# The end of a fused model kernel: two norm weight rows loaded narrow and spread by TensorE, three more weight chunks loaded in halves, a scatter moved between two halves, and a table load moved ahead of a branch

## The reference

```
h = layer_norm(DEEPNORM_ALPHA * h + t, ln_g[i, 0], ln_b[i, 0])
f = moe_ffn(h, ...)        # 32 experts, 4 chosen for each token
h = layer_norm(DEEPNORM_ALPHA * h + f, ln_g[i, 1], ln_b[i, 1])

# one expert, for the rows that chose it:
h = xb @ w_gu[e] + b_gu[e]                      # 1024 -> 2048, gate and up
h_gate, h_up = jnp.split(h, 2, axis=-1)
act = min(h_gate, 7) * sigmoid(1.702 * min(h_gate, 7)) * (clip(h_up, -7, 7) + 1.0)
y = act @ w_down[e] + b_down[e]                 # 1024 -> 1024
```

## Time and profile before

| what | value |
|---|---|
| median of 3 runs | 2072.09 us (2069.9 to 2073.24) |
| span of the profiled execution, first to last instruction | 2072.4 us |
| device time of the profiled execution | not listed apart from its span |
| PE busy | 1989.1 us, 96% of the span |
| DVE, ACT, POOL busy | 43%, 33%, 2% |
| DMA read from HBM | 601.71 MB |

### The profile page before, as it was taken

The page is one execution under the profiler, slowest core; times in us unless marked ns, Lnnn a source line. Parts: engine busy times, 40 slices in busy tenths (PEclk is TensorE's granted clock), DMA queues, the critical chain, the costliest instruction groups (busy, mean ns, idle before and its releaser), DMA issues.

```text
span 2072.4 us, 28104 instructions
## 1 busy us (share of the span) xinstructions
PE 1989.1 (96%) x12146; PEld 1377.3 (66%) x12146; DVE 897.4 (43%) x1078; ACT 688.3 (33%) x949; POOL 39.1 (2%) x30
## 2 busy tenths in 40 slices
PE   8999999999999998999999999999999999999997
PEld 8998768999999886999888544443334333434433
DVE  6766666676666787666644311111111111111102
ACT  5546475545555565444344111110101010101101
POOL 0700000000000000000000000000000000000000
PEclk9999999999999998999999999999999999999999
DMA  9663707556556442555387999999999999999997
GB/s 311 202 218 135 234 1 256 191 184 201 171 189 208 166 159 79 171 199 183 100 294 292 371 427 428 428 428 427 427 428 427 427 428 428 427 428 428 427 428 308
DMA packets 165592, 604.26 MB, mean 292 GB/s; under 512 B 9324, under 2 KB 102464, under 8 KB 140564
## 3 DMA queue, kind: packets, MB, share of 16 engines
q1 hardware_dynamic: 165328, 602.79, 74.9%
q10 hardware_dynamic: 164, 0.04, 0.0%
HBM read 601.71 MB, written 1.09 MB: 291 GB/s over the span
## 4 chain that ended last, share of the span: by engine, by line
PE 69%; DMA 22%; DVE 4%; ACT 3%; issue 1%; SPq 0%; DVEq 0%; ACTq 0%
PE ps L1794 14%; PE ps L1796 14%; PE ps L1795 14%; PE ps L2332 11%; PE ps L2356 6%; DMA sb_raw<-in_moe_w_gate_up 5%; DMA sb_raw<-in_moe_w_down 5%; DMA sb_w_free<-in_moe_w_gate_up 3%; DMA sb_late_raw<-in_moe_w_down 3%; DMA sb_nat_more<-in_moe_w_gate_up 3%; PE ps L2302 2%; DMA sb_w_free<-in_moe_w_down 2%; ACT sb_w_hi L663 1%; DVE sb_w_lo L1084 1%; PE ps L2364 1%; PE ps L2313 1%
## 5 line engine op out<-in xcount | busy, mean ns | idle before, releaser
L1084 DVE TENSOR_TENSOR sb_w_lo<-sb_raw,sb_w_hi 128x2048 fp32r<-128x2048 f32 x175 | 403.0, 2311 | 239.4 <-ACT sb_w_hi L663 238.9
L663 ACT ACTIVATE sb_w_hi<-sb_raw 128x2048 fp32r<-128x2048 f32 x179 | 340.5, 1912 | 168.8 <-PE ps L1796 155.2
L1794 PE MATMUL ps<-sb_xT_hi,sb_w_hi 128*128 128x256 f32 x1344 | 373.3, 278 | 0.0
L1795 PE MATMUL ps<-sb_xT_lo,sb_w_hi 128*128 128x256 f32 x1344 | 372.7, 277 | 0.0
L1796 PE MATMUL ps<-sb_xT_hi,sb_w_lo 128*128 128x256 f32 x1344 | 372.7, 277 | 0.0
L1795 PEld LDWEIGHTS ps<-sb_xT_lo,sb_w_hi 128*128 128x128 f32 x1344 | 253.0, 188 | 1.5
L1794 PEld LDWEIGHTS ps<-sb_xT_hi,sb_w_hi 128*128 128x128 f32 x1344 | 252.3, 188 | 1.7 <-DVE sb_w_lo L1084 0.2
L1796 PEld LDWEIGHTS ps<-sb_xT_hi,sb_w_lo 128*128 128x128 f32 x1344 | 253.1, 188 | 0.0
L1672 DVE COPY sb_h_rows<-ps 128x512 f32<-128x512 f32 x31 | 21.4, 692 | 318.3 <-PE ps L2332 318.3
L1003 ACT ACTIVATE sb_h_rows<-ps 128x512 f32<-128x512 f32 x32 | 19.2, 599 | 420.4 <-PE ps L2332 420.4
L1794 PE MATMUL ps<-sb_w_hi,sb_xT_hi 128*128 128x512 f32 x384 | 153.6, 400 | 0.3 <-DVE sb_xT_lo L1113 0.2
(11 more groups left out here) (314 smaller groups left out, 2541.1 us busy)
## 6 DMA issues: line engine op xcount, KB each, us to landing
sb_raw<-in_moe_w_gate_up SPq DMA_DIRECT2D x49, 2048.0 KB, 34.6
sb_w_free<-in_moe_w_gate_up SPq DMA_DIRECT2D x46, 2048.0 KB, 34.6
sb_raw<-in_moe_w_down SPq DMA_DIRECT2D x23, 2048.0 KB, 34.0
sb_raw<-in_ffn_w_up SPq DMA_DIRECT2D x44, 1024.0 KB, 5.4
sb_raw<-in_ffn_w_down SPq DMA_DIRECT2D x44, 1024.0 KB, 5.1
sb_w_free<-in_moe_w_down SPq DMA_DIRECT2D x22, 2048.0 KB, 33.8
sb_raw<-in_ffn_w_gate SPq DMA_DIRECT2D x43, 1024.0 KB, 5.5
sb_late_raw<-in_moe_w_gate_up SPq DMA_DIRECT2D x17, 2048.0 KB, 32.5
```

Of the source, the lines that this page charges most:

```text
L663: sc.activation(w_hi[:, c % CUT, :], raw[:, c % RAW, :], ACT.Copy).then_inc(hi_made, 1)
L1084: ve.tensor_tensor(w_lo[:, c % CUT, :], raw[:, c % RAW, :], w_hi[:, c % CUT, :].bitcast(F32), ALU.subtract).then_inc(lo_made, 1)
L1794: pe.matmul(o, l_hi, r_hi, start=start, stop=False)
L1795: pe.matmul(o, l_hi, r_lo, start=False, stop=False)
```

## The change

- The two weight rows of the last layer norm are loaded as two DMAs of 4 KB each into partitions 64 and 65 of a tile `narrow_rows`, whose first 32 partitions now hold `down_bias`. They are issued right behind `down_bias`, long before the experts end. The two 512 KB DMAs, and the wait in front of them, go.
- TensorE spreads a row over all partitions by a matmul of K = 2 with a broadcast column of `ident` (`spread_last_rows`): the gain into banks 2 and 3 between chunks t+1 and t+2, the bias into banks 0 and 1 behind the branch. ScalarE copies the spread gain to `xs_even` (128x1024), and the next `turn_picks` waits for that copy. The bias is read from PSUM by VectorE, which waits for it in front of the second pass of the first 128 tokens.
- Chunks t+3, t+4 and t+5 are loaded as two DMAs of 1 MB each, and TensorE waits for the halves apart.
- The scatter of expert 30 moves from behind chunk t+6 to between its halves.
- `warm(ACT.Sqrt)` moves from behind ScalarE's branch to ahead of it.

```diff
 # SP, last_loads
-                for j in range(4):
+                for j in range(3):
                     expert_chunk("gate_up", N_E - 1, j, t + j, laps)
-                for j in range(2):
-                    expert_chunk("down", N_E - 2, j, t + 4 + j, laps)
+                sp.wait_ge(chunk_used, used_no(t + 3, laps) - RING)
+                sp.dma_start(dst[:, 0:1, :], src[:, 0:1, :]).then_inc(last_gate_row, 16)
+                sp.dma_start(dst[:, 1:2, :], src[:, 1:2, :]).then_inc(slot_loaded[(t + 3) % RING], 16)
...
+                sp.dma_start(dst[:, 0:2, :], src[:, 0:2, :]).then_inc(down_rows_0, 16)
+                sp.dma_start(dst[:, 2:4, :], src[:, 2:4, :]).then_inc(slot_loaded[(t + 4) % RING], 16)
...
+                sp.dma_start(dst[:, 0:2, :], src[:, 0:2, :]).then_inc(down_rows_1, 16)
+                sp.dma_start(dst[:, 2:4, :], src[:, 2:4, :]).then_inc(slot_loaded[(t + 5) % RING], 16)
 # SP, behind the router's logits
-            sp.dma_start(down_bias[:], a["moe_b_down_2"][0]).then_inc(down_bias_loaded, 16)
+            sp.dma_start(down_bias, a["moe_b_down_2"][0]).then_inc(down_bias_loaded, 16)
+            sp.dma_start(ln1_rows[0:1, :], a["ln_g_2"][0, 1:2]).then_inc(ln1_loaded, 16)
+            sp.dma_start(ln1_rows[1:2, :], a["ln_b_2"][0, 1:2]).then_inc(ln1_loaded, 16)
 # SP, behind all chunks
-            sp.wait_ge(chunk_used, ROUND_C * more + (MOE_C0 + KEPT_T[1] + 1))
-            sp.dma_start(ln1_gain, rows(a["ln_g_2"][0, 1], D)).then_inc(ln1_loaded, 16)
-            sp.dma_start(ln1_bias, rows(a["ln_b_2"][0, 1], D)).then_inc(ln1_loaded, 16)
 # VectorE, last_layer_norm
+                ln1_bias = ps[:, 0:2, :].rearrange("p a b -> p (a b)")
-                ve.wait_ge(ln1_loaded, 16 * 2)
+                ve.wait_ge(gain_copied, more + 1)
                 ve.scalar_tensor_tensor(out=x[:, 0, :], in0=rows(0), scalar=mean_var[:, 0, 0:1], in1=ln1_gain,
...
+                ve.wait_ge(bias_spread, 1)
                 ve.scalar_tensor_tensor(out=x[:, 0, :], in0=x[:, 0, :], scalar=stat[:, 6:7], in1=ln1_bias,
 # TensorE
+            def spread_last_rows(row, bank):
+
+                one = ident[2 * N_E:2 * N_E + 2, 2 * N_E + row:2 * N_E + row + 1].to_broadcast([2, SLOTS])
+                for h in range(2):
+                    for half in halves:
+                        ins = pe.matmul(ps[half, bank + h, :], one, ln1_rows[:, 512 * h:512 * (h + 1)], start=True, stop=True)
+                return ins
...
             with pe.If(more > 0):
                 with pe.Fori(1, more + 1) as r:
                     another_round(r)
+            spread_last_rows(1, 0).then_inc(bias_spread, 1)
```

More of the change, by code:

```diff
@@ L163, in build @@
         late = ExitStack()
-        down_bias = sb("down_bias", [N_E, D], stack=late)
+        narrow_rows = sb("narrow_rows", [P, D], stack=late)
+        down_bias, ln1_rows = narrow_rows[0:N_E, :], narrow_rows[2 * N_E:2 * N_E + 2, :]
         y_part = ExitStack()
@@ L228, in build @@
         m_sig, m_u, m_u_last = gate_part, up_part, up_last
-        ln1_gain, ln1_bias = kept_more[:, 0, 0:D], kept_more[:, 0, D:2 * D]
+        ln1_gain = xs_even[:].rearrange("p k e s -> p (k e s)")
         halves_of = lambda t: t.rearrange("p (k n) -> p k n", k=2)
@@ L307, in build @@
         out_stored, third_row = sem("out_stored"), sem("third_row")
+        last_gate_row, down_rows_0, down_rows_1 = sem("last_gate_row"), sem("down_rows_0"), sem("down_rows_1")
+        gain_spread, gain_copied, bias_spread = sem("gain_spread"), sem("gain_copied"), sem("bias_spread")
         last_sum, last_mean = sem("last_sum"), sem("last_mean")
@@ L888, in last_layer_norm @@
             def last_layer_norm(more):
-                rows, unread = ps[:, 6:8, :].rearrange("p a b -> p (a b)"), xs_even[:].rearrange("p k e s -> p (k e s)")
+                rows, unread = ps[:, 6:8, :].rearrange("p a b -> p (a b)"), kept_0[:, 0:D]
                 sc.wait_ge(last_scattered, 4 * more + 4)
@@ L1036, in last_two @@
                 turned_picks(e, 0)
+                sc.wait_ge(gain_spread, r + 1)
+                sc.activation(ln1_gain, ps[:, 2:4, :].rearrange("p a b -> p (a b)"), ACT.Copy).then_inc(gain_copied, 1)
                 sc.wait_ge(m_act_made, e + 1)
@@ L1043, in last_two @@
                 turned_picks(e + 1, 1)
+                warm(ACT.Sqrt)
             def last_outputs(r):
@@ L1073, in _ @@
                     another_round(r)
-            warm(ACT.Sqrt)
             last_outputs(more)
@@ L2323, in bias, with gate_up_rows @@
                               bias_parts[:, col + 512 * h:col + 512 * (h + 1)], start=True, stop=False)
-            def gate_up_rows(left, t, j, laps, r):
-                pe.wait_ge(slot_loaded[t % RING], loaded_no(t, laps, r))
+            def gate_up_rows(left, t, j, laps, r, in_halves=False):
+                if in_halves:
+                    pe.wait_ge(last_gate_row, 16 * (r + 1))
+                else:
+                    pe.wait_ge(slot_loaded[t % RING], loaded_no(t, laps, r))
                 for k in range(2):
+                    if in_halves and k == 1:
+                        pe.wait_ge(slot_loaded[t % RING], loaded_no(t, laps, r))
                     for bank in range(2):
@@ L2337, in _, with down_rows @@
             last_own = lambda i: m_u_last.rearrange("p (t h s) -> p t h s", t=4, h=2)[:, i % 4, i // 4, :]
-            def down_rows(t, j, laps, r, in_parts=False, own=own, bank=2, in_halves=False):
+            def down_rows(t, j, laps, r, in_parts=False, own=own, bank=2, first_half=None, between=None):
                 if t in KEPT_T:
                     pe.wait_ge(kept_loaded[j], (32, 16)[j])
-                elif in_halves:
-                    pe.wait_ge(ahead_rows, 16 * (r + 1))
+                elif first_half is not None:
+                    pe.wait_ge(first_half, 16 * (r + 1))
                 elif not in_parts:
@@ L2347, in down_rows @@
                 for k in range(4):
-                    if in_halves and k == 2:
+                    if between and k == 2:
+                        between()
+                    if first_half is not None and k == 2:
                         pe.wait_ge(slot_loaded[t % RING], loaded_no(t, laps, r))
@@ L2478, in last_two @@
                 turn_picks(QUADS * r, s)
-                for j in range(1, 4):
-                    gate_up_rows(left, t + j, j, laps, r)
+                gate_up_rows(left, t + 1, 1, laps, r)
                 pe.wait_ge(pickT_made, e + 1)
+                pe.wait_ge(m_act_made, e + 1)
+                pe.wait_ge(ln1_loaded, 16 * 2)
+                spread_last_rows(0, 2).then_inc(gain_spread, 1)
+                gate_up_rows(left, t + 2, 2, laps, r)
+                gate_up_rows(left, t + 3, 3, laps, r, in_halves=True)
+                pe.wait_ge(gain_copied, r + 1)
                 turn_picks(QUADS * r, s + 1)
-                pe.wait_ge(m_act_made, e + 1)
-                down_rows(t + 4, 0, laps, r)
+                down_rows(t + 4, 0, laps, r, first_half=down_rows_0)
                 pe.wait_ge(gate_read, e + 2)
@@ L2488, in last_two, with scatter_here @@
                 turn_rows(up_last, 1)
-                down_rows(t + 5, 1, laps, r)
+                down_rows(t + 5, 1, laps, r, first_half=down_rows_1)
                 pe.wait_ge(m_act_made, e + 2)
-                down_rows(t + 6, 0, laps, r, own=last_own, bank=0, in_halves=True)
-                pe.wait_ge(y_lo_made, e + 1)
-                scatter().then_inc(scattered, 1)
+                def scatter_here():
+                    pe.wait_ge(y_lo_made, e + 1)
+                    scatter().then_inc(scattered, 1)
+                down_rows(t + 6, 0, laps, r, own=last_own, bank=0, first_half=ahead_rows, between=scatter_here)
                 down_rows(t + 7, 1, laps, r, True, last_own, 0)
```

9 lines of the change are left out of this document (8 added, 1 removed).

## The result

| | before | changed |
|---|---|---|
| median of 14 runs each | 2072.78 us (2069.9 to 2078.01) | 2079.08 us (2076.9 to 2085.04) |
| ratio to before, 95% interval | | 1.0029 (1.0021 to 1.0036) |
| span of the profiled execution | 2072.4 us | 2076.4 us |
| its device time | | 2078.33 us |

The change makes the kernel slower by 0.29%, 6.0 us by the ratio. The forecast was 2073.9 us with a range up to 2076.4, so it was wrong, in size and in its verdict: slower by over 0.2% had a chance of 0.09. About 1.9 us of the device time lie outside the span. By that the profiled execution of before, with its span of 2072.4 us, took about 2074.3 us, which is 2.2 us over the median of 2072.09 and not 0.3. The forecast adds a difference to the median and is untouched by this.

A forecast was written before the change was run, and what follows sets the result against it. Over the last 40 us the weight loads set the pace, and TensorE can gain only its lag behind them. −1.05 us in front plus 2.9 of bias wait gives +1.85; from the median 2072.09, 2073.9 us, range 2070.6 to 2076.4.

The forecast's parts named there:

- The wide loads go, the narrow ones come: Norm-row loads: the wide ones hold no chunk up, the narrow 8 KB fall into a nearly idle DMA time; 0.
- The spread of the gain: Four matmuls between t+1 and t+2: 1.7 us of work, given back by reading t+3 in halves; 0 on the path.
- rival C: Follow-up run's rival, no chance given: TensorE bounds the whole tail, so 1.9 us less work ends up to 0.9 us earlier.
- Halves: Chunks t+3 to t+5 loaded as 1 MB pieces: last landing +0.2 us, bounded between −0.3 and +0.3.
- Rival 4: Loads of t+3 to t+5: 1 MB pieces are dear, landing 3.9 us later, end at +4.7 to +6.5; chance 0.02.
- TensorE behind the landings: End of t+7: with halves and the moved scatter, TensorE follows its landings and ends at 2059.7, not 2060.30; −0.6 us.
- The table load: ScalarE, table load ahead of its branch: last `y_hi` starts 0.14 us behind t+7 instead of 0.58; −0.45 us.
- The sum: Whole kernel: −1.05 + 2.9 = +1.85 us, with ends +1.0 and +2.75.
- The gain in front: Last `y_hi`, last scatter and all behind them come 0.6 + 0.45 = 1.05 us earlier, if nothing new is waited for.
- The bias behind the branch: VectorE's second pass waits for four bias matmuls behind TensorE's branch: +2.1 us at full clock to +3.8 at lower, 2.9 taken.
- Rival 3: Behind TensorE's branch: code fetched in two steps, a second delay of 3.5 us, +4.5 to +6.3 in all; chance 0.06.

The follow-up runs named there:

- experiment 1: Changed kernel with the bias spread right behind TensorE's last scatter, ahead of its branch: 2072.94 us, ratio to before 0.9995.
- experiment 7: Changed kernel with the bias spread ahead of TensorE's branch and the gain loaded wide again: 2072.94 us, ratio to before 0.9992.
- experiment 4: Kernel before with only the square root's table load moved ahead of ScalarE's branch: 2073.56 us, ratio to before 0.9999.
- experiment 6: Kernel before with only chunks t+3 to t+5 in halves and the scatter between the halves of t+6: 2073.72 us, ratio to before 0.999.
- experiment 2: Changed kernel with four never-run matmuls of padding in the body that TensorE's branch skips: 2076.07 us, ratio to before 1.0015.
- experiment 3: Kernel before with only the bias row loaded narrow and spread behind TensorE's branch: 2077.34 us, ratio to before 1.0022.
- experiment 5: Changed kernel with 62 never-run matmuls of padding in the body that TensorE's branch skips: 2078.06 us, ratio to before 1.0018.
- experiment 9: Changed kernel with the body skipped by TensorE's branch cut to four transposes, bias spread still behind it: 2071.45 us, ratio to before 0.9986.
- experiment 8: Changed kernel with the bias spread ahead of TensorE's branch, the same kernel measured a second time: 2073.62 us, ratio to before 0.9994.

## Why the prediction was wrong, step by step

- **The wide loads go, the narrow ones come: 0.** Right. The narrow ones were issued at 1142.81 and 1143.14, and SP's next load came 9 us later. That the wide ones held nothing up is seen in experiments 1 and 7.
- **The spread of the gain: 0.** Right at the end (experiment 7). In between it pushes t+2 back, as foreseen: in experiment 1 t+2 had landed at 2032.15 and was taken at 2033.41, behind the spread, and TensorE waited for a landing again at t+6, for 0.22 us. But it is not right in every execution. In the changed kernel's profile t+2 had landed at 2030.8 and was taken at 2033.50, and TensorE waits for no chunk from there to the end of t+7, so the spread's 1.9 us lie on its path. Without it t+7 could have ended 1.2 us behind the last landing, at 2056.8 and not at 2057.64: an estimate of 0.9 us lost, from the seven profiles in the table. That is experiment 7's rival C, in this one execution.
- **Halves: +0.2.** Right as far as can be told. From the landing of t+2, whole in every kernel, to the last are 24.7 us in experiment 1 (2032.15 to 2056.86) and in the changed kernel, against 24.5 before and 24.65 in experiment 4 (2038.71 to 2063.36): 0.1 to 0.2 us for three chunks, with landings read to 0.1 us. Rival 4, with 3.9 us, is out.
- **TensorE behind the landings: −0.6.** Right. The forecast had t+7 end about 1.2 us behind its last landing, 0.8 closer than before, less the 0.2 by which that landing moves. Seven profiles have 1.16 to 1.23 us where the three with whole chunks and the old scatter have 1.87 to 1.98. Which of the two edits brings it, the halves or the scatter, no run tells. The changed kernel's own profile, with 2.07, is the exception. TensorE does the same work there as in experiment 1 at the same places to within 0.1 us until the end of t+5 (t+2 starts at 2033.50 and 2033.41), and the stretch at the low clock is as long, but the chunks land 1.3 us earlier, and TensorE stays behind them to the end. Why they land earlier there is open.
- **The table load: −0.45.** Right alone (experiment 4). Beside the moved scatter the edit is worth nothing (experiment 6): with the scatter in its new place ahead of it, `y_hi` starts 0.05 behind t+7 without the edit. The sum counts it once and holds, but the reason was another. The gain in front is then about 0.7 plus the 0.3 to 0.5 between t+7 and `y_hi`, which either edit gives: 1.0 to 1.2, near the forecast's 1.05.
- **The bias behind the branch: +2.1 to +3.8.** This is the step that failed. The branch (3.6 us), the low clock, the start of the spread behind it and the queue behind VectorE's wait were right, and experiments 2 and 3 gave 3.3 and 3.8. Wrong was "They begin at 2065.0 and take 2 × 0.86 + 0.2 = 1.93 us at the full clock", to 3.65 at the lower: that the four matmuls come as one piece. They straddled the end of a block of code, and the second block came 3.3 us behind the first. First start to last end was 2069.83 − 2062.88 = 6.95 us.
- **The chances.** Rival 3 named this mechanism with its price, +4.5 to +6.3, and got 0.06. My evidence against it was that "the single instruction that ran behind it came at once". One instruction cannot show what happens to eight. That 3.6 us for one jump was unexplained spoke for fetching, and once code is fetched in blocks the open question is whether the eight records lie in one. With blocks of 256, as experiment 5 took them, 16 instructions at a random place lie across the end of one in 15 of 256 cases, an estimate of 0.06 too; so the number was not absurd, but I did not know why. The place is not random: it is fixed by the program, and a count of TensorE's instructions might have settled the case before any run. I did not try that.

**What the gaps consist of.** The windows of the queue for instructions, cut into stretches of 0.05 us, say when each fetch of the changed kernel starts: at 2060.15 and at 2063.45. The shares above (2.0% of 16 engines over 3.6 us, 2.2% over 3.3 us) make 1.15 us for each. So the first gap is about 1.0 us from the start of the branch to the start of the fetch, 1.15 us of fetch, and 1.6 us more until the matmuls run. The second is 0.6 us from the first matmul to the next fetch, 1.2 us of fetch, and 1.5 us more. In experiment 5 the second fetch also starts 0.6 us behind the first piece (2065.05 against 2064.49). The second block is not asked for together with the first, and that is why the two delays add up.

**Still open.** What the sequencer does in the 1.5 us between the end of a fetch and the first instruction, no row says. The near branch's kernel measured 2.9 us under before where the sum gives 1.05. Its profile has the same 12.8 us behind the last landing as experiment 1, so the rest lies ahead of that or is chance; the interval reaches to −0.2 and holds both.

## What to carry to other kernels

Nothing that another engine waits for should stand first behind a jump over a long body: put it ahead of the branch, where it cost nothing here, with only 0.2 us to spare in one profile, or keep the jump short. When work does stand there, count the instructions that have to be fetched and price the gap twice, since any edit of the program, even of code that never runs, can move the block's end into the middle of it. And when two edits relieve the same wait, take the gain of one: look at what the first leaves for the second.

## What the runs showed of the hardware

- TensorE's compare-and-branch took 204 ns to a target four transposes on (experiment 9), and 3367 to 3679 ns over a whole round (the ten other profiles, experiments 2 and 4 at the ends).
- Behind a far jump the instructions up to a block's end ran at once, the rest 3.28 to 3.38 us behind the start of the first piece (the changed kernel and experiment 5). Moving the code by 16 instructions or by 248 moved the split as blocks of 256 instructions would. The Trainium skill, "Runtime: NRT & Kernel Launch", Instruction fetch mechanics, gives that size, as 16 KiB. The trace agrees: 2 and 6 records against 6 and 2, and 16.4 KB for each packet of the queue (1.23 MB in the changed kernel's 75).
- Four fp32 matmuls of 64x512 took 1.93 us at full clock (experiments 7, 8 and 9) and 3.67 us at the low one (experiment 3). The clock fell ahead of the spread or during it in all four kernels with the spread behind a far jump, and in one of the four without (experiment 1, 2.68 us). When it falls is not tied to the jump: in experiment 2 it was still full at the jump's end and fell at 2063.3. That the idle time of the jump lowers it is likely, not shown.
